# Thirty-two bytes less behind the vector table: where the tiles of a four-sublayer trunk begin in SBUF

## The chip, the cores and the metric

The kernel runs on one core of a Trainium2 chip. What counts is the device time of one execution in microseconds. Below, PE is TensorE's matmul row, PEld its weight-load row, DVE is VectorE, ACT is ScalarE, POOL is GpSimd and SP is the engine that issues most DMAs. SBUF has 128 partitions, and an address in this text is a byte offset within one partition.

## The reference

Two residual layers over a sequence of 1024 tokens with 1024 channels, each with a token mixer and then an MLP of hidden width 4096:

```python
for i in range(DEPTH):                      # DEPTH = 2
    hn = rmsnorm(x, mix_pre_g[i])
    if i % 2 == 0:
        y = pool_mixer(hn, pool_w[j], pool_b[j], pool_scale[j])
    else:
        y = mlstm_mixer(hn, ...)            # 8 heads of 128, chunkwise
    x = x + rmsnorm(y, mix_post_g[i])
    hn = rmsnorm(x, ffn_pre_g[i])
    a = relu(hn @ mlp_w1[i])                # 1024 -> 4096
    y = (a * a) @ mlp_w2[i]                 # 4096 -> 1024
    x = x + rmsnorm(y, ffn_post_g[i])
```

All arrays are float32. Nearly all arithmetic lies in the two MLPs and in the input and output projections of the mLSTM mixer.

## The kernel before, in words

Channels lie on partitions and tokens along the free dimension, in two halves of T = 512 tokens. A product of a 128x128 weight tile with a 128x512 activation tile is made in three **rounded** matmuls. Both operands are split into a high part, rounded to the type float32r, and a low part, the rest, of the same type; the products high·high, weight high with activation low, and weight low with activation high are added in one PSUM bank:

```python
c = row + cols_of(k)
a, b = w_hi[:, c:c + P], w_lo[:, c:c + P]
nc.tensor.matmul(o, a, hi(t), start=(k == 0), stop=False)
nc.tensor.matmul(o, a, lo(t), start=False, stop=False)
last = nc.tensor.matmul(o, b, hi(t), start=False, stop=(k == n - 1))
```

The first operand behind the output is the stationary one (the weights, loaded by a weight load of its own before every matmul), the second is the moving one: 512 columns of 4 bytes, 2048 bytes of each partition in one unbroken run. The same three-matmul pattern stands in `three_passes` (lines 803 to 805, most projections of the mLSTM and the pooling map), `plain_first` (903 to 905), `plain_second` (926 to 928), `pairs_first` (970 to 972, the first MLP matrix as a Strassen-like product of seven), `second` (1020 to 1022, the second MLP matrix likewise), and in the output projection (867 to 869 and 1040 to 1042).

ACT makes the high parts by casts, DVE the low parts by a subtraction, each one step ahead of PE; semaphores keep the order. A ring of four 512-column rows in `w_hi` and `w_lo` holds the weights. SP loads weights into `raw`, `raw_odd` and the `w2` tiles. PE's program order is written out by hand.

A smaller number of matmuls are **plain** float32 ones: the windows of the pooling mixer (line 837), sums of squares with a matrix of ones (785, 792, 814, 1188), transposes (1076, 1090, 1093, 1132), the attention-like products of the mLSTM (1096, 1107, 1118, 1122), and additions through the identity at the end (1196, 1199). A plain float32 matmul leaves two records on PE in the profile, a rounded one leaves one.

**Where the tiles lie.** Tiles are placed in SBUF one behind the other in the order in which they are made, and each takes its size rounded up to a multiple of 32 bytes. The first ones are, in order:

```python
y = [sb(f"y{h}", [P, KT, T]) for h in range(HALVES)]
raw = sb("raw", [P, RAW * BLK])
w_hi = sb("w_hi", [P, ROWS * T], F32R)
w_lo = sb("w_lo", [P, ROWS * T], F32R)
vecs = sb("vecs", [P, VECS])
consts = sb("consts", [P, CONSTS])
...
eps = sb("eps", [P, 1])
```

`y0`, `y1`, `raw`, `w_hi` and `w_lo` begin at 8320, 24704, 41088, 49280 and 57472, all multiples of 64 (of 128, too). `vecs` (169 columns, 676 bytes, in a place of 704) begins at 65664, and `consts` at 66368, also multiples of 64. `eps`, one column of 4 bytes in a place of 32, begins at 68928, and so everything behind it begins at 32 more than a multiple of 64, from `early_h` and `h_plain` (68960) over `x11_hi` (90080), `x11_lo` (98272) and the other activation tiles `x.._hi` and `x.._lo` to `hid_hi` and `hp_hi` (155616), `h_hi` (196576) and `h_lo` (202720). The exceptions stand behind smaller odd-sized tiles: `ssq`, `rs`, `prob` (210176), `hnorm`, `state`, `rows`, `cols` and `small` begin at multiples of 64. All moving operands of all rounded matmuls are slices of 2048 bytes in tiles that begin at 32 more than a multiple of 64. All their stationary operands, in `w_hi` and `w_lo`, begin at multiples of 64.

Of the plain matmuls, the moving operand is `consts` in the transposes and `y` in line 1199 (multiples of 64), and `x_last`, `qT`, `relu_sq`, `win`, `inter_b` and `sq` (32 more) in lines 1196, 1096, 785 and 837. A name in the profile stands as output<-moving,stationary; `state` in line 837 begins at a multiple of 64 as well.

Of the kernel before, what the change touches and what calls it, by code (L numbers as in the profile page):

```python
# [13 lines left out]
P = 128  # L14
# [71 lines left out]
VECS = 169  # L86
# [157 lines left out]
def build(nc, x_in, x_tokens, weights, w_first, w_second, vecs_in, consts_in, bands_in, out):  # L244
# [9 lines left out]
    with ExitStack() as ctx:  # L254
        def sb(name, shape, dt=F32):
            return ctx.enter_context(nc.sbuf_tensor(name, shape, dt))
# [9 lines left out]
        raw = sb("raw", [P, RAW * BLK])  # L266
        w_hi = sb("w_hi", [P, ROWS * T], F32R)
        w_lo = sb("w_lo", [P, ROWS * T], F32R)
        vecs = sb("vecs", [P, VECS])
        consts = sb("consts", [P, CONSTS])  # L270
        ident = consts[:, C_IDENT:C_IDENT + P]
        mask = consts[:, C_MASK:C_MASK + T]
        eps = sb("eps", [P, 1])

        with ExitStack() as shared:
            h_plain = shared.enter_context(nc.sbuf_tensor("h_plain", [P, 2, T], F32))
# [2261 lines left out]
```

## Time and profile before

| | |
|---|---|
| median of 2 runs | 1941.2 us (1939.57 to 1942.83) |
| span of the profiled execution, first to last instruction | 1938.4 us |
| median less that span | 2.8 us |
| granted TensorE clock | 1.000 of full |
| PE, PEld, DVE, ACT busy | 99%, 79%, 69%, 55% of the span |
| chain that ended last | PE 90%, DVE 6%, issue 2%, ACT 2% |

The profile does not give a time of the profiled execution beside its span; the runs' times are taken from outside the program, so the 2.8 us hold what lies around the span and the difference of one execution from another. A sum made against the span is carried over to the median by adding them. Matmuls are pipelined, and their ends in the profile are modelled: the time that one takes from the others is the distance from its start to the next start, not its duration.

### The profile page before, as it was taken

The page shows a single profiled execution, that of the slowest core. Times are in us where ns is not written, and L with a number is a line of the kernel's source. Part 1 is how long each engine was busy: PE and PEld are TensorE (multiplying, and loading weights), DVE is VectorE, ACT ScalarE, POOL GpSimd, SP SyncE. Part 2 cuts the span into 40 slices and gives each one's busy share as a digit, 9 for nine tenths or more (in the row PEclk, how much of TensorE's full clock was granted, in tenths as well). Part 3 has the DMA queues.
Part 4 walks back from the last instruction along what each step waited for, and adds up shares of the span by engine and source line. Part 5 has one row for each costly group of instructions (what it writes and reads, how often), then busy time and mean ns, then how long its engine had stood idle before and what let it go on. Part 6 is the DMA issues. An engine that isn't in the chain of part 4 may idle for free.

```text
span 1938.4 us, 24458 instructions
## 1 busy us (share of the span) xinstructions
PE 1914.3 (99%) x8526; PEld 1534.2 (79%) x8526; DVE 1344.2 (69%) x2120; ACT 1068.5 (55%) x1825; POOL 89.8 (5%) x121
## 2 busy tenths in 40 slices
PE   9999999999999999999999999999999999999999
PEld 6678888888788788888878878777888888878876
DVE  5877565655678987786866868777665656577875
ACT  7655545454445537766766757655555555444533
POOL 0110000000000200010000100020000000000010
PEclk9999999999999999999999999999999999999999
DMA  5344343448633533352323442245243436753353
GB/s 211 122 152 161 120 166 134 159 172 320 218 93 95 181 123 103 109 169 93 99 86 98 133 150 88 77 157 190 77 179 120 179 120 250 281 179 94 108 190 125
DMA packets 79706, 285.00 MB, mean 147 GB/s; under 512 B 9408, under 2 KB 9536, under 8 KB 71136
## 3 DMA queue, kind: packets, MB, share of 16 engines
q1 hardware_dynamic: 64288, 239.96, 35.2%
q0 software_dynamic: 8320, 27.27, 4.3%
q10 hardware_dynamic: 6976, 16.21, 2.7%
q8 instruction: 69, 1.13, 0.3%
q14 instruction: 53, 0.43, 0.1%
HBM read 211.51 MB, written 71.89 MB: 146 GB/s over the span
## 4 chain that ended last, share of the span: by engine, by line
PE 90%; DVE 6%; issue 2%; ACT 2%; DMA 0%; SPq 0%; DVEq 0%; ACTq 0%
PE bank L803 7%; PE bank L805 6%; PE bank L804 6%; PE core L1020 5%; PE core L1021 5%; PE core L1022 5%; PE core L972 5%; PE core L971 5%; PE core L970 5%; PE bank L1020 4%; PE bank L1022 4%; PE bank L1021 4%; PE bank L972 4%; PE bank L971 4%; PE bank L970 4%; PE bank L903 2%
## 5 line engine op out<-in xcount | busy, mean ns | idle before, releaser
L1467 ACT CAST h_hi<-h_raw 128x512 fp32r<-128x512 f32 x188 | 116.5, 620 | 246.7 <-PE core L1022 149.1
L1831 DVE TENSOR_TENSOR w_lo<-raw,w_hi 128x1024 fp32r<-128x1024 f32 x132 | 161.3, 1223 | 125.5 <-ACT w_hi L1281 123.4
L803 PE MATMUL bank<-x_hi,w_hi 128*128 128x512 f32 x560 | 227.3, 406 | 2.9 <-issue 2.5
L1281 ACT CAST w_hi<-raw 128x1024 fp32r<-128x1024 f32 x132 | 137.9, 1045 | 156.9 <-PE bank L805 48.5
L805 PE MATMUL bank<-x_hi,w_lo 128*128 128x512 f32 x560 | 221.8, 396 | 0.0
L804 PE MATMUL bank<-x_lo,w_hi 128*128 128x512 f32 x560 | 220.6, 394 | 0.0
L2088 DVE TENSOR_TENSOR h_lo<-h_raw,h_hi 128x512 fp32r<-128x512 f32 x188 | 129.7, 690 | 120.8 <-ACT h_hi L1467 120.5
L1020 PE MATMUL core<-h_hi,w_hi 128*128 128x512 f32 x464 | 183.8, 396 | 0.6 <-DVE y L2154 0.6
L1021 PE MATMUL core<-h_lo,w_hi 128*128 128x512 f32 x464 | 183.4, 395 | 0.0
L1022 PE MATMUL core<-h_hi,w_lo 128*128 128x512 f32 x464 | 183.0, 394 | 0.0
L1982 DVE TENSOR_TENSOR w_lo<-sums,w_hi 128x512 fp32r<-128x512 f32 x104 | 71.8, 690 | 100.4 <-ACT w_hi L1309 97.5
L1020 PE MATMUL bank<-h_hi,w_hi 128*128 128x512 f32 x336 | 132.9, 395 | 0.0
L1021 PE MATMUL bank<-h_lo,w_hi 128*128 128x512 f32 x336 | 132.8, 395 | 0.0
L1022 PE MATMUL bank<-h_hi,w_lo 128*128 128x512 f32 x336 | 132.5, 394 | 0.0
L2126 DVE TENSOR_TENSOR w_lo<-w,w_hi 128x512 fp32r<-128x512 f32 x174 | 123.6, 711 | 11.1 <-ACT w_hi L1483 6.7
L803 PEld LDWEIGHTS bank<-x_hi,w_hi 128*128 128x128 f32 x560 | 105.3, 188 | 27.5 <-issue 5.2
L805 PEld LDWEIGHTS bank<-x_hi,w_lo 128*128 128x128 f32 x560 | 105.1, 188 | 25.5
L804 PEld LDWEIGHTS bank<-x_lo,w_hi 128*128 128x128 f32 x560 | 105.3, 188 | 23.9 <-issue 0.7
L1483 ACT CAST w_hi<-w 128x512 fp32r<-128x512 f32 x174 | 107.1, 615 | 12.3 <-DVE w L2106 4.6
L1309 ACT CAST w_hi<-sums 128x512 fp32r<-128x512 f32 x104 | 64.7, 622 | 82.1 <-PE core L972 37.9
L1020 PEld LDWEIGHTS core<-h_hi,w_hi 128*128 128x128 f32 x464 | 87.1, 188 | 23.2 <-issue 2.2
L1022 PEld LDWEIGHTS core<-h_hi,w_lo 128*128 128x128 f32 x464 | 87.1, 188 | 21.4
(334 smaller groups left out, 4397.5 us busy)
## 6 DMA issues: line engine op xcount, KB each, us to landing
raw<-weights SPq DMA_DIRECT2D x132, 512.0 KB, 3.3
h_pair_dram<-y SPq DMA_DIRECT2D x26, 1792.0 KB, 6.6
h_raw<-h_pair_dram SPq DMA_DIRECT2D x182, 256.0 KB, 2.8
w<-second_pairs SPq DMA_DIRECT2D x24, 768.0 KB, 4.5
raw_odd<-first_pairs SPq DMA_DIRECT2D x14, 1024.0 KB, 7.2
x_scratch<-y POOLq DMA_DIRECT2D x48, 256.0 KB, 2.4
raw<-first_pairs SPq DMA_DIRECT2D x12, 1024.0 KB, 7.1
xold<-x_scratch POOLq DMA_DIRECT2D x40, 256.0 KB, 3.4
```

What stands on the lines that cost most here:

```text
L803: nc.tensor.matmul(o, a, hi(t), start=(k == 0), stop=False)
L804: nc.tensor.matmul(o, a, lo(t), start=False, stop=False)
L805: last = nc.tensor.matmul(o, b, hi(t), start=False, stop=(k == n - 1))
L970: nc.tensor.matmul(o, a, xh[:, k, :], start=(fresh and k == 0), stop=False, skip_group_check=True)
L971: nc.tensor.matmul(o, a, xl[:, k, :], start=False, stop=False, skip_group_check=True)
L972: last = nc.tensor.matmul(o, b, xh[:, k, :], start=False, stop=(final and k == 3), skip_group_check=True)
L1020: nc.tensor.matmul(o[:, :], a, hh, start=(fresh and first), stop=False, skip_group_check=True)
L1021: nc.tensor.matmul(o[:, :], a, hl, start=False, stop=False, skip_group_check=True)
L1022: ins = nc.tensor.matmul(o[:, :], b, hh, start=False, stop=(final and last), skip_group_check=True)
L1281: nc.scalar.copy(w_hi[:, ROW[u] * T:(ROW[u] + 2) * T], raw[:, (n % RAW) * BLK:(n % RAW + 1) * BLK]).then_inc(hi_ready, 1)
L1831: dve.tensor_tensor(w_lo[:, s], raw[:, (n % RAW) * BLK:(n % RAW + 1) * BLK], w_hi[:, s].bitcast(F32), ALU.subtract).then_inc(lo_ready, 1)
L2088: dve.tensor_tensor(lo, h_raw[:, at % H_RAW, :], hi.bitcast(F32), ALU.subtract).then_inc(h_lo_ready, 1)
```

## The change

`eps` loses its tile and becomes the 170th column of the vector table. 170 columns are 680 bytes, which still take a place of 704, so `consts` stays where it is, and every tile behind the place of `eps` begins 32 bytes lower.

```diff
         w_lo = sb("w_lo", [P, ROWS * T], F32R)
-        vecs = sb("vecs", [P, VECS])
+        vecs_eps = sb("vecs", [P, VECS + 1])
+        vecs, eps = vecs_eps[:, 0:VECS], vecs_eps[:, VECS:VECS + 1]
         consts = sb("consts", [P, CONSTS])
         ident = consts[:, C_IDENT:C_IDENT + P]
         mask = consts[:, C_MASK:C_MASK + T]
-        eps = sb("eps", [P, 1])
```

After it `early_h` begins at 68928, `x11_hi` at 90048, `hid_hi` at 155584, `h_hi` at 196544 and `h_lo` at 202688: all multiples of 64. `y`, `raw`, `w_hi`, `w_lo`, `vecs` and `consts` stay. `ssq`, `rs`, `prob`, `hnorm`, `state`, `rows`, `cols` and `small`, which began at multiples of 64, begin at 32 more. On PE, DVE, ACT, POOL and SP the same instructions stand in the same order with the same waits; only the address of what they read and write differs, and what read `eps` (the biases of the square roots, and the memset at line 1259) now names `vecs`.

## Rows read from the trace of the kernel before

**Rows 1.** The page: busy time and share of each engine; the chain that ended last.
```profile
PE 1914.3 (99%) x8526; PEld 1534.2 (79%) x8526; DVE 1344.2 (69%) x2120; ACT 1068.5 (55%) x1825; POOL 89.8 (5%) x121
...
PE 90%; DVE 6%; issue 2%; ACT 2%; DMA 0%; SPq 0%; DVEq 0%; ACTq 0%
```

**Rows 2.** The longest wait of PE by releaser: us, times, longest.
```profile
PE bank L803 <- issue: 3.5, 4, 1.5
```

**Rows 3.** PE's instructions with w_lo, whole span: us, busy (count), clock, DMA share, GB/s.
```profile
0.00:1938.50 1938.50, 1001.95 (x2528) 1.00 0.43 147
```

**Rows 4.** The same of PE's instructions with w_hi.
```profile
0.00:1938.50 1938.50, 1596.14 (x5056) 1.00 0.43 147
```

**Rows 5.** Timeline of PE from 600.76: start us, us, engine line op tiles.
```profile
600.76 0.39 PE L1020 MATMUL bank<-h_hi,w_hi 128*128 128x512 f32 x1
...
604.96 0.39 PE L1020 MATMUL bank<-h_hi,w_hi 128*128 128x512 f32 x1
```

**Rows 6.** PE in two long stretches, columns as in group 3.
```profile
150.00:600.00 450.00, 450.00 (x1929) 1.00 0.46 166
1350.00:1700.00 350.00, 350.00 (x1501) 1.00 0.47 175
```

**Rows 7.** Timeline of PE at the program's end, plain float32, 512 columns.
```profile
1925.43 0.59 PE L1196 MATMUL bank<-x_last,consts 128*128 128x512 f32 x1
1925.86 2.74 PE L1196 MATMUL core<-x_last,consts 128*128 128x512 f32 x6
1928.43 2.81 PE L1199 MATMUL bank<-y,consts 128*128 128x512 f32 x6
...
1930.22 1.02 PE L1199 MATMUL bank<-y,consts 128*128 128x512 f32 x2
```

**Rows 8.** Timeline of PE, plain float32, 128 columns.
```profile
809.41 0.60 PE L1090 MATMUL core<-consts,kT 128*128 128x128 f32 x4
809.85 0.60 PE L1093 MATMUL core<-consts,vT 128*128 128x128 f32 x4
810.28 1.06 PE L1096 MATMUL core<-qT,kT 128*128 128x128 f32 x8
```

**Rows 9.** Timeline of PE in the pooling windows.
```profile
18.23 0.38 PE L837 MATMUL core<-sq,y 128*128 128x128 f32 x2
```

**Rows 10.** Groups by form: line, tiles, count | busy us, mean ns of one | idle before.
```profile
L1096 PE MATMUL core<-qT,kT 128*128 128x128 f32 x128 | 16.9, 275 | 0.0
...
L1090 PE MATMUL core<-consts,kT 128*128 128x128 f32 x64 | 9.6, 273 | 0.1
```

**Rows 11.** Timeline of PE from 700.01.
```profile
700.01 0.40 PE L1020 MATMUL core<-h_hi,w_hi 128*128 128x512 f32 x1
700.25 0.39 PE L1021 MATMUL core<-h_lo,w_hi 128*128 128x512 f32 x1
700.48 0.39 PE L1022 MATMUL core<-h_hi,w_lo 128*128 128x512 f32 x1
700.71 0.40 PE L1020 MATMUL core<-h_hi,w_hi 128*128 128x512 f32 x1
```

**Rows 12.** Groups by form of the first MLP matrix, columns as in group 10.
```profile
L972 PE MATMUL core<-x_hi,w_lo 128*128 128x512 f32 x224 | 89.4, 399 | 0.0
L971 PE MATMUL core<-x_lo,w_hi 128*128 128x512 f32 x224 | 88.2, 394 | 0.0
L970 PE MATMUL core<-x_hi,w_hi 128*128 128x512 f32 x224 | 87.8, 392 | 0.0
```

**Rows 13.** PE's instructions with w_lo where PE has gaps, columns as in group 3.
```profile
0.00:112.00 112.00, 34.91 (x88) 1.00 0.49 173
1250.00:1315.00 65.00, 31.93 (x81) 1.00 0.42 140
```

**Rows 14.** Busy PE, PEld, DVE, ACT and POOL (count of each), clock, DMA share, GB/s.
```profile
629.70:648.80 19.10, 19.10 (x83) 15.39 (x82) 18.30 (x23) 9.13 (x16) 5.29 (x5) 1.00 0.45 135
...
600.00:700.00 100.00, 99.69 (x427) 79.91 (x427) 87.37 (x124) 49.85 (x86) 14.97 (x18) 1.00 0.48 150
```

## The prediction, made before the changed kernel ran

> **What bounds the kernel now.** I began with the engines' busy times and the chain of waits [rows 1]: PE is busy for 99% of the span and the chain that ended last runs through PE for 90% of it, with 6% on DVE and 2% on ACT. The waits of PE by their releaser [rows 2] are short, 3.5 us for the longest group. So a change that makes a matmul shorter is paid out nearly in full, and one that touches another engine's work hardly at all.
>
> Next I counted. Every rounded matmul reads either `w_lo` or `w_hi`: 2528 [rows 3] and 5056 [rows 4] records, 7584 in all, of 8526 on PE. All have 512 columns, and all have a moving operand whose place the change moves from 32 beyond a multiple of 64 bytes to a multiple of 64.
>
> Then the time that one takes, from start to start. From 600.76 to 604.96 us there are 18 steps between starts [rows 5]: 4.20 us / 18 = **233.3 ns**. The long stretches agree: 450 us hold 1929 and 350 us hold 1501 rounded matmuls [rows 6], 233.3 and 233.2 ns, at a granted clock of 1.00, which is the 2.4 GHz level. 7584 x 233.3 ns = 1769 us of the 1938.4 us span. This is the figure that the change can move, and it does not depend on what ACT, DVE or the DMAs do beside it, since it holds over stretches with very different neighbours.
>
> What should it be? The plain float32 records give a measure. With 512 columns they follow each other at 2.57 us / 6 = 429 ns [rows 7] (1925.86 to 1928.43), with 128 columns at 0.44 us / 4 = 109 ns [rows 8]. The difference, 320 ns for 384 columns, is 0.833 ns a column, two cycles of 2.4 GHz, and some 2.4 ns remain for each record whatever its length. A rounded matmul that takes one cycle a column would need 512 x 0.4167 + 2.4 = **215.7 ns**. It takes 233.3 ns, **17.6 ns** more. The plain ones, which load weights for every record as well, show no such surplus. The question of this case is how much of those 17.6 ns comes from where the moving operand begins.
>
> The page "TensorE: Matmul & The Clock Gate" of the Trainium skill (Part 2 and Back-to-back issue gap) gives the gap at full clock as columns / 2.4 plus 2.5 ns, about 216 ns here, with the weights read through a port of their own. The trace agrees for the plain records (two cycles a column in place of one) and does not for the rounded ones, at 233.3 ns; the page names no cause for such a surplus.
>
> **The change, part by part.**
>
> *The moving operands of 7584 rounded matmuls go from 32 to 0 modulo 64.* No row shows a rounded matmul with a moving operand at a multiple of 64, so the cost is bounded from both sides. The bound of most gain is the whole surplus, 17.6 ns each: 7584 x 17.6 = 133.5 us. The bound of no gain comes from the plain records: `x_last` (32 modulo 64) and `y` (0 modulo 64) as moving operands, both against `consts`: 429 ns, and 1.02 us for two records less the 0.59 us that the last one lasts, 430 ns [rows 7]. With 128 columns, `sq` (32 modulo 64) takes 0.38 less 0.27, some 110 ns, beside 109 for `consts` (0 modulo 64) [rows 8 to 10]. The place makes no difference there. But plain records take a column in two cycles, and so ask for their 2048 bytes at half the rate: a lost read could hide in them and not in a rounded matmul.
>
> Between these ends one value has a mechanism that the rows suggest. The starts in a trio of rounded matmuls are not even: 0.24, 0.23, 0.23 us from 700.01 to 700.71 [rows 11], and in the first MLP matrix one of the three is always longer, 399 ns beside 392 and 394 [rows 12]. The slip is 5 to 7 ns, and 16 columns x 0.4167 = 6.67 ns: 16 columns of 4 bytes are 64 bytes. 233.3 ns is 560 cycles, 35 times 16. So I read the stream as coming in blocks of 64 bytes, at one block for 16 cycles. A run of 2048 bytes that begins on a block touches 32 of them, and one that begins in the middle of a block touches 33. The change would then take one block of 35 from each rounded matmul, **6.67 ns**, leaving 226.7 ns. This is an estimate; the two blocks that stay (switching weights, or what else) have nothing to do with the place. 7584 x 6.67 = **50.6 us**.
>
> I take this value, though the nearest row by kind is the plain one with no difference, because the plain ones run at half the rate, and the excess of the rounded ones appears exactly where the read rate is doubled.
>
> *What is not paid out.* Up to 112 us, and from 1250 to 1315 us, PE has gaps and ends on ACT's and DVE's steps; there stand 3 x (88 + 81) = 507 rounded matmuls [rows 13], whose gain I count as lost: 507 x 6.67 = 3.4 us. From 629.7 to 648.8 us DVE is busy for 18.30 of 19.10 us [rows 14], and the same stretch comes back in the second MLP. PE could be 2.9% faster there, 0.55 us, twice 0.55 is 1.1 us; DVE leaves 0.8 us of room, so it would be just enough, but waits between engines stand in the way, and I count it as lost. In the wider stretch, 600 to 700, DVE has 87.37 us in 100 [rows 14], enough room. Elsewhere DVE and ACT work at 69% and 55% of the span, and a PE that is 2.9% faster brings them to 71% and 57%.
>
> *The tiles that go from 0 to 32 modulo 64* (`prob`, `hnorm`, `state`, `rows`, `cols`, `small`): moving or stationary operands of plain matmuls, and operands of DVE and ACT. By the plain rows above, nothing; `qT` against `kT`, both at 32, shows the largest difference of any plain pair: (1.06 - 0.275) / 7 = 112 ns against 109 [rows 8, 10]. If all 942 other records became 3 ns longer it would be 2.8 us; `state` and `prob` stand in a quarter of them, so at most 0.7 us. I take 0, and keep that in the range.
>
> *`eps` inside `vecs`*: the same instructions with the same waits; its memset and the load of the other 169 columns touch different bytes. Nothing.
>
> **The sum**, against the profiled execution: 1938.4 - 50.6 + 3.4 + 1.1 = 1892.3 us of span, and with the 2.8 us between span and median 1895.1. **1895 us**, 2.4% less.
>
> **The rivals.**
>
> *A, no difference.* The surplus of 17.6 ns belongs to the rounded format or to the switch of weights, and the place of the moving operand is as indifferent as in the plain records [rows 7]. The time would be 1941 us. For it speaks that every pair of plain records that differs in the place alone takes the same time, and that the rounded matmuls switch weights at every step. Against it: the plain ones switch weights as often, even at 109 ns [rows 8], without a surplus. The page "SBUF — State Buffer" of the Trainium skill (Specifications) gives lines of 16 bytes; with lines of 16, or of 32, both places begin on a line, and the change would do nothing, which is this rival's 1941 us. No run shown here tells a line's length.
>
> *B, the whole surplus goes.* Each block of 64 bytes that is cut in two costs something, not only the one at the end, and a run on the blocks streams at one column a cycle. 7584 x 17.6 = 133.5 us, less 507 x 17.6 = 8.9 us where PE waits, and less what DVE then holds back: in each of the two dense stretches of 19.1 us PE would want 1.4 us and DVE leaves 0.8 [rows 14], and waits of PE for DVE that are hidden today come out at stage ends, some 3 us in all by the size of those in [rows 2]. 1941.2 - 133.5 + 8.9 + 3 = 1819.6, **1820 us**. For it: 215.7 ns is what the plain records lead to. Against it: nothing explains 42 cycles by one misplaced start, and the slip that the trace shows is some 16 cycles.
>
> *C, slower.* The stationary operands `w_hi` and `w_lo` begin at multiples of 64, and now the moving ones do too. If the weight load for the next matmul and the moving stream meet in the same half of the same block at the same time, each matmul loses a block: 7584 x 6.67 = +50.6 us, **1992 us**. It decides from 5.1 ns a matmul on (2% of 1941 over 7584). Against it stand `y` against `consts`, both at multiples of 64, with 430 ns [rows 7], no more than `x_last`, and `consts` with 109 ns [rows 8]; for it, that `qT` and `kT`, which share their place modulo 64, are the only pair at 112.
>
> **How the numbers follow.** The block estimate 0.36, A 0.33, B 0.24, C 0.07. The likeliest gives 1895 us. A measurement of this kernel can tell about 2% from no change, so the limits are 1902 and 1980 us. The block estimate and B are faster; I leave 0.02 of the first for the case that more is held back than 4.5 us: faster 0.58, within 2% 0.35, slower 0.07. The range reaches from B with some 5 us less held back, 1815 us, to A with the 0.7 us of the moved small tiles and the spread of the runs, 1946 us; it leaves out C and a little of B. The likeliest case alone has 1885 to 1902 us. It is wide because the price of one nanosecond a matmul is 7.6 us, and no row of this trace shows a rounded matmul at the other place.
>
> **What would show each step right or wrong.** In the changed kernel's timeline the distance between starts of rounded matmuls in long stretches answers everything: 226.7 ns (450 us would hold 1985) for the block estimate, 233.3 (1929) for A, 215.7 (2086) for B, 240 (1875) for C. If the trio's uneven steps are gone, the reading by blocks is supported. The plain records should stay at 429 and 109 ns; if `x_last` gets shorter, the plain ones depend on the place too. PE's waits should grow only before 112 us, around 630 to 650 and around 1250 to 1315 us, and by less than 5 us. I would be wrong as a whole if the distance fell and the time did not: then DVE or ACT would be the bound in more places than [rows 14] shows.

## The result, and the profile after

| | before | changed |
|---|---|---|
| median of 2 runs | 1941.2 us (1939.57 to 1942.83) | 1916.7 us (1916.18 to 1917.21) |
| span of the profiled execution | 1938.4 us | 1914.4 us |
| ratio of the times | | 0.9877, 95% interval 0.986 to 0.9894 |

The changed kernel is 1.2% faster, 24.5 us. The forecast was 1895 us with a range of 1815 to 1946. The direction was right; about half of the gain came.

The page of the changed kernel, busy times and chain, beside [rows 1]:

```profile
PE 1883.8 (98%) x8526; PEld 1535.6 (80%) x8526; DVE 1343.7 (70%) x2120; ACT 1067.9 (56%) x1825; POOL 89.8 (5%) x121
...
PE 87%; DVE 8%; issue 2%; ACT 2%; DMA 0%; SPq 0%; DVEq 0%; ACTq 0%
```

DVE's and ACT's busy times are the same to 0.6 us. All of the change is on PE. Its long stretches, beside [rows 6] (us, busy and count, clock, DMA share, GB/s):

```profile
150.00:590.00 440.00, 439.96 (x1922) 1.00 0.47 170
1340.00:1660.00 320.00, 320.00 (x1399) 1.00 0.45 170
```

440 us / 1922 is 228.9 ns and 320 / 1399 is 228.7 ns (the counts take in a matmul or two at the edges). From the starts themselves a rounded matmul now takes 229.0 ns, where it took 233.3: **4.3 ns less**, not 6.67. The timeline of the changed kernel shows it too, beside [rows 5]:

```profile
592.38 0.39 PE L1020 MATMUL bank<-h_hi,w_hi 128*128 128x512 f32 x1
...
595.81 0.39 PE L1020 MATMUL bank<-h_hi,w_hi 128*128 128x512 f32 x1
```

Fifteen steps, 3.43 us, 228.7 ns each. The uneven steps within a trio, which were to go if the reading by blocks was right, are still there: 226, 229 and 232 ns in turn, where before they were 231, 232 and 237. The plain records stay as they were: `x_last` from 1901.83 to 1904.41 us has six in 2.58 us, 430 ns each, and the transposes of line 1090 take 0.44 us for four. But one kind of rounded matmul did not gain, and that is the line of this trace to stop at. `early_h` too begins at a multiple of 64 now:

```profile
430.66 0.39 PE L1020 MATMUL bank<-early_h,w_hi 128*128 128x512 f32 x1
...
432.75 0.40 PE L1020 MATMUL bank<-early_h,w_hi 128*128 128x512 f32 x1
```

Nine steps of PE in 2.09 us are 232 ns; the trios of such matmuls lasted 699 to 701 ns before and last 697 to 703 now, while those with any other tile went from 700 to 687. Seventy-two matmuls are worth nothing in the time, but they say that a start at a multiple of 64 is not enough.

### The profile page after: what moved, and what is told of

The parts are those of the page before. It is cut to its first block, busy times and chain, and to the rows that moved or that the text cites. A ratio compares the mean times of both kernels' runs of the same rounds, so it can differ in the third digit from the quotient of the medians.

```text
span 1914.4 us, 24458 instructions
## 1 busy us (share of the span) xinstructions
PE 1883.8 (98%) x8526; PEld 1535.6 (80%) x8526; DVE 1343.7 (70%) x2120; ACT 1067.9 (56%) x1825; POOL 89.8 (5%) x121
## 3 DMA queue, kind: packets, MB, share of 16 engines
q8 instruction: 69, 1.13, 0.3%
## 4 chain that ended last, share of the span: by engine, by line
PE 87%; DVE 8%; issue 2%; ACT 2%; DMA 0%; SPq 0%; DVEq 0%; ACTq 0%
PE bank L803 6%; PE bank L805 5%; PE bank L804 5%; PE core L1020 5%; PE core L1022 5%; PE core L1021 5%; PE core L971 5%; PE core L970 5%; PE core L972 5%; PE bank L1020 4%; PE bank L1022 4%; PE bank L1021 4%; PE bank L971 4%; PE bank L970 4%; PE bank L972 4%; PE bank L903 2%
## 5 line engine op out<-in xcount | busy, mean ns | idle before, releaser
L1021 PEld LDWEIGHTS core<-h_lo,w_hi 128*128 128x128 f32 x464 | 87.1, 188 | 19.2
```

What stands on the lines that cost most here:

```text
L1021: nc.tensor.matmul(o[:, :], a, hl, start=False, stop=False, skip_group_check=True)
```

## The experiments

**1. Where must a moving operand begin?** The trunk is left out of this kernel; each case has a line of its own, for instance

```diff
+ [mm(bank[0][:, 0:512], W(128 + (z == 2) * 8192, 128 * (j % 4)), M(64 + (z == 1) * 8192, 512),
+     start=(j == 0 and z == 0), stop=(j == 15 and z == 2)) for j in range(16) for z in range(3)]
```

where `W` and `M` slice the weights and the moving operand at a byte offset, both counted from a multiple of 2048.

> This kernel leaves the whole trunk out (it copies its input to its output) and only times matmuls, each case in its own line: trios of rounded 128x512 matmuls as in the kernel (weights high with moving high, weights high with moving low, weights low with moving high, the low parts 8192 bytes behind the high ones, weights stepping by 512 bytes from 128 beyond a multiple of 2048), with the moving operand beginning 0, 32, 64 to 2016 bytes beyond a multiple of 2048; then the stationary operand moved, fewer columns, starts off multiples of 32, one operand pair repeated, plain float32 and bfloat16. Theory 1 (multiples of 64 decide): 229 ns a matmul at every even multiple of 32, 233.3 at every odd one, whatever the place in 2048. Theory 2 (where the 2048-byte run crosses a boundary of 2048 decides, since the tiles that gained begin 64 bytes before one and early_h, which begins 1344 beyond one, did not gain): 233 to 234 ns over most of the 64 places, 229 only near 1984, and something else again at 0, where nothing is crossed. Theory 3 (a clash of the moving stream with the weight load): the time changes when only the stationary operand is moved. Per-column or per-matmul: with 128, 256 and 384 columns the surplus over columns x 0.4167 ns stays at 15 to 18 ns if it is a price of the matmul, and shrinks in proportion if it is one of the columns. Plain float32 429 ns at each place.

The timeline of that kernel (start us, us, line, tiles, count). Lines 53 to 61 have the moving operand at 0, 32, 64 to 256, with the weights at 128; the distance between two starts over 48 is the time of one matmul:

```profile
38.17 11.32 PE L53 MATMUL bank<-mov,wts 128*128 128x512 f32 x48
49.33 11.40 PE L54 MATMUL bank<-mov,wts 128*128 128x512 f32 x48
60.57 11.37 PE L55 MATMUL bank<-mov,wts 128*128 128x512 f32 x48
71.77 11.36 PE L56 MATMUL bank<-mov,wts 128*128 128x512 f32 x48
82.97 11.07 PE L57 MATMUL bank<-mov,wts 128*128 128x512 f32 x48
93.87 11.37 PE L58 MATMUL bank<-mov,wts 128*128 128x512 f32 x48
105.08 11.16 PE L59 MATMUL bank<-mov,wts 128*128 128x512 f32 x48
116.07 11.37 PE L60 MATMUL bank<-mov,wts 128*128 128x512 f32 x48
127.28 11.36 PE L61 MATMUL bank<-mov,wts 128*128 128x512 f32 x48
```

At 0 and 64, both multiples of 64, a matmul takes 11.16 / 48 = 232.5 and 11.20 / 48 = 233.3 ns; at 128 it takes 10.90 / 48 = 227 ns; at 192, where the changed kernel's tiles lie if whole multiples of 256 are left out, 10.99 / 48 = 229 ns. The pattern comes back every 256 bytes up to 2016, within about 1 ns (the start at 256 has 233.5 where that at 0 has 232.5). So theories 1 and 2 fall: what counts is neither a multiple of 64 nor the boundary of 2048. In the second part only the weights are moved, under a moving operand that stays:

```profile
751.12 11.06 PE L117 MATMUL bank<-mov,wts 128*128 128x512 f32 x48
762.02 11.35 PE L118 MATMUL bank<-mov,wts 128*128 128x512 f32 x48
773.21 11.36 PE L119 MATMUL bank<-mov,wts 128*128 128x512 f32 x48
784.41 11.40 PE L120 MATMUL bank<-mov,wts 128*128 128x512 f32 x48
...
883.75 11.08 PE L129 MATMUL bank<-mov,wts 128*128 128x512 f32 x48
894.67 11.35 PE L130 MATMUL bank<-mov,wts 128*128 128x512 f32 x48
```

Lines 117 to 120 have the moving operand at 0 and the weights at 0, 32, 64 and 96: 227, 233, 233, then 234 ns. Line 129 has both at 32, at no multiple of 64, and takes 10.92 / 48 = 227 ns. Theory 3 is left, that the two operands' places act together. For starts at multiples of 32 what counts is the **distance, start of the moving operand less start of the weights, modulo 256**. By it all of the kernel's rows fall into place: 96 before (233.4 ns), 64 after (228.8 here, 229.0 in the whole kernel), and for `early_h` 224 before and 192 after (233.3 both). Means of the middle spacings of each case, from the starts of both this kernel and the one of experiment 3:

```
distance modulo 256   0      32     64     96     128           160    192    224
ns a matmul           226.7  233.3  228.8  233.4  232.4, 233.5  234.3  233.3  233.3
```

At distance 128 the two values come from different starts in the first kernel; the start at 256 gave 233.5 there and 232.4 in the other, so 1 ns can hang on what ran before.

Two kinds showed no dependence at the places tried. Plain float32 at 0, 32 and 1984 (distances 128, 160 and 64), lines 191 to 193, and bfloat16, line 195:

```profile
1506.31 20.76 PE L191 MATMUL bank<-mov,wts 128*128 128x512 f32 x48
1526.91 20.76 PE L192 MATMUL bank<-mov,wts 128*128 128x512 f32 x48
1547.51 20.76 PE L193 MATMUL bank<-mov,wts 128*128 128x512 f32 x48
...
1588.93 10.31 PE L195 MATMUL bank<-mb,wb 128*128 128x512 bf16 x47
```

20.60 / 48 = 429.2 ns at each, and 215.8 ns for bfloat16. Plain float32 was not tried at distance 0.

The question per column or per matmul got neither of its two answers: the surplus over columns x 0.4167 ns was 58 ns with 128 columns (111.7 ns at every place tried), 7 to 13 with 256 and 13 to 17 with 384. With 256 columns the good distance is another one. Line 170 has distance 192:

```profile
1290.63 5.61 PE L170 MATMUL bank<-mov,wts 128*128 128x256 f32 x48
1296.08 8.61 PE L171 MATMUL bank<-mov,wts 128*128 128x384 f32 x48
```

That is 5.45 / 48 = 113.5 ns, where distance 0 takes 120.0 (experiment 3).

**2. The same in the whole kernel.** Three placements, each with all of the trunk and nothing else changed. In the first, on the kernel before, `eps` goes ahead of `w_hi`, so that the weights move and no moving tile does:

```diff
+        eps = sb("eps", [P, 1])
         w_hi = sb("w_hi", [P, ROWS * T], F32R)
...
         consts = sb("consts", [P, CONSTS])
...
-        eps = sb("eps", [P, 1])
```

> The kernel before with eps ahead of w_hi in place of behind consts: the weights begin 32 bytes higher and every moving tile stays where it was, 32 beyond a multiple of 64. Theory 'multiples of 64': nothing is gained, 233.3 ns a rounded matmul, 1941 us. Theory 'distance' (what counts is the start of the moving operand less the start of the stationary one, modulo 256: 96 before, 64 in the changed kernel): the distance is now 64, so 229 ns and 1917 us, as the changed kernel.

In the second, on the changed kernel, the tiles stay at multiples of 64 and the distance is made a bad one:

```diff
+        pool_bs = sb("pool_bs", [P, KT])
+        ssq = sb("ssq", [P, 2, HALVES * CPH])
+        rs = sb("rs", [P, HALVES * CPH])
         w_hi = sb("w_hi", [P, ROWS * T], F32R)
...
         ones = sb("ones", [P, P])
-        pool_bs = sb("pool_bs", [P, KT])
-        ssq = sb("ssq", [P, 2, HALVES * CPH])
-        rs = sb("rs", [P, HALVES * CPH])
```

> The changed kernel with pool_bs, ssq and rs (128 bytes) ahead of w_hi: the moving tiles of the arena stay where the change put them, at multiples of 64, and the weights too are at multiples of 64, 128 bytes higher. Theory 'multiples of 64': 229 ns, 1917 us as the changed kernel. Theory 'distance': it is 192 modulo 256, at which the scan had 233.3 ns, so 1941 us as before.

In the third, also on the changed kernel, it is made 0 for all, `early_h` included: `ssq` alone ahead of `w_hi`, `pool_bs` and `rs` ahead of `early_h`.

> The changed kernel with ssq (64 bytes) ahead of w_hi and pool_bs and rs (64 bytes) ahead of early_h: all moving tiles of rounded matmuls, early_h too, have the distance 0 modulo 256 to the weights. Theory 'distance': 226.7 ns a rounded matmul, 2.3 ns less than the changed kernel, 7584 x 2.3 = 17 us, less what PE's waits take back: 1900 us. Theory 'multiples of 64': 1917 us.

And in a fourth, run later, 0 for all with no operand at a multiple of 64: `eps` and `ssq` ahead of `w_hi`, on the kernel before, and `pool_bs` and `rs` ahead of `early_h`.

> The kernel before with eps and ssq (96 bytes) ahead of w_hi, and pool_bs and rs (64) ahead of early_h: the distance of every moving tile of a rounded matmul to the weights is 0 modulo 256, as in e_same256, but weights and moving tiles all begin 32 beyond a multiple of 64. If the distance alone counts: 226.7 ns and 1901 us, as e_same256. If starts at multiples of 64 give anything beside it: more than that, up to 1941 us.

| kernel | starts modulo 64: weights, moving | distance | us | ratio to before, 95% interval |
|---|---|---|---|---|
| before | 0, 32 | 96 | 1940.0 (with the first three), 1939.8 (with the fourth) | |
| changed | 0, 0 | 64 | 1916.7 | 0.9877 (0.986 to 0.9894) |
| eps ahead | 32, 32 | 64 | 1914.5 | 0.9866 (0.985 to 0.9883) |
| 128 bytes ahead | 0, 0 | 192 | 1939.9 | 1.0005 (0.9996 to 1.0015) |
| all at 0 | 0, 0 | 0 | 1901.4 | 0.9804 (0.9789 to 0.9818) |
| all at 0, odd | 32, 32 | 0 | 1902.7 | 0.9808 (0.9791 to 0.9824) |

The changed kernel's row is that of the first section, beside a before of 1941.2 us.

Each of the four came out within 3 us of what the distance gave and against what multiples of 64 gave. The windows say the same in counts. With 128 bytes ahead:

```profile
150.00:600.00 450.00, 450.00 (x1929) 1.00 0.45 165
```

which is the very count of [rows 6], and with all at distance 0:

```profile
150.00:590.00 440.00, 439.93 (x1941) 1.00 0.47 168
```

440 / 1941 = 226.7 ns. `early_h` gains there as well (the second line below is the first matmul of another tile, and five steps lie between the two, 1.13 us, 226 ns each):

```profile
426.65 0.39 PE L1021 MATMUL bank<-early_h,w_hi 128*128 128x512 f32 x1
...
427.78 0.39 PE L1020 MATMUL bank<-h_hi,w_hi 128*128 128x512 f32 x1
```

The kernel with all at 0 is 2.0% faster than before. It is the version to keep: 1901.4 us stand against the changed kernel's 1916.7, though the two were not timed side by side; the intervals of their ratios to before do not touch.

**3. What is it that meets?** A second kernel of matmuls alone:

> Only matmuls, as in the first scan; the trunk is left out. (a) The distance from stationary to moving start in steps of 8 bytes from 0 to 248: 226.7 ns at 0, 229 at 64 and 233 to 234 at most others, if the scan's values hold. (b) Two weights in turn, with distance 0 to the moving operand of their own matmul and 32 or 224 to that of the matmul before, during which they are loaded, and the reverse: if the load of the next weights clashes with the running stream, the pair with distance 0 to the next weights takes 226.7 and the other 233; if a matmul's own weights count, the reverse. (c) 96, 64 and 32 weight columns: if the surplus comes from the weight load beside the stream, it shrinks with the columns loaded, towards 215.8 ns, and so does its dependence on the distance; if it is a price of the rounded format or of switching weights, it stays. (d) Weights 2048, 4096 and 6144 bytes further: no change. (e) 256 to 448 columns: the dependence on distance is the same number of ns at each.

(a) held in the main: 226.7 ns at 0, 228.8 at 64 and 233 to 234 at most others. Finer distances gave values between and beyond: 230.0 ns at 56, 104 and 248, 240.0 at 120 and 236.7 at 240. The 240 of the timeline, line 68, beside its neighbours at 112 and 128:

```profile
206.08 11.25 PE L67 MATMUL bank<-mov,wts 128*128 128x512 f32 x48
217.17 11.68 PE L68 MATMUL bank<-mov,wts 128*128 128x512 f32 x48
228.68 11.31 PE L69 MATMUL bank<-mov,wts 128*128 128x512 f32 x48
```

(11.51 / 48 = 239.8 ns.) Nothing was faster than distance 0. Off the multiples of 32 the period of 256 is not clean: at distance 112 this kernel has 231.1 ns, with the moving operand 240 beyond a multiple of 2048, and the first one 226.7, with it at 2032; at 120 they have 240.0 and 234.3. Tiles begin at multiples of 32, so the trunk does not meet these. (d) held: weights 2048, 4096 and 6144 bytes further take 226.7 ns each. (c) fell in its first part. With fewer weight columns the surplus did not shrink towards 215.8 ns:

```profile
463.26 11.20 PE L90 MATMUL bank<-mov,wts 128*96 128x512 f32 x48
474.30 11.04 PE L91 MATMUL bank<-mov,wts 128*96 128x512 f32 x48
...
573.85 11.28 PE L100 MATMUL bank<-mov,wts 128*32 128x512 f32 x48
584.97 11.34 PE L101 MATMUL bank<-mov,wts 128*32 128x512 f32 x48
```

With 96 columns it is distance 0 that takes 230.0 ns (line 90, 11.04 / 48) and distance 32 that takes 226.7 (line 91); with 32 columns 231.7 and 233.3. What did shrink is the dependence on the distance. Over the same five distances (0, 32, 64, 96 and 160) the values run from 226.7 to 234.3 ns with 128 weight columns, from 226.7 to 233.3 with 96, from 228.4 to 231.4 with 64 and from 230.5 to 233.3 with 32. So the surplus does not come down with the weights loaded, but how many are loaded changes how much the distance matters and which distance is the good one. (e), the same number of ns at each length, fell. In ns, at distances 0, 64 and 96:

```
columns    256     320     384     448     512
at 0       120.0   146.7   173.3   202.6   226.7
at 64      117.8   146.7   173.3   200.0   228.8
at 96      119.9   146.7   176.7   205.3   233.4
columns x 0.4167
           106.7   133.3   160.0   186.7   213.3
```

At 320, 384, 448 and 512 columns the lowest is columns x 0.4167 + 13.3 ns, 32 cycles of 2.4 GHz for each rounded matmul. It is no floor for every length: 256 columns go down to 113.3 ns (mean of line 170's middle spacings), 6.7 above 106.7. What comes on top of the 13.3 ns in this table is 0 to 7 ns, and hangs on the distance at 384, 448 and 512 columns and not at 320. At 448 columns distance 64 is better than 0. (b), whether a matmul's own or the next weights belong to its distance, was not decided: 231.7 ns for one order and 230.0 for the other. A third kernel asked again:

> Only matmuls, the trunk is left out. Weights and moving operand change in turn, 128 bytes beyond a multiple of 256 or x more, to see which two starts belong together. If a matmul's time hangs on its moving operand and its own weights: the cases with own distance 0 give 226.7 for each x. If on the moving operand and the next weights: those with next distance 0 do. If on both, or on the moving operand after: neither does, as in the two cases of the scan before (231.7 and 230.0). The moving operand alternating over the same weights, and the weights over one moving operand, should then lie between the values at the two distances. bfloat16 over eight distances: 215.8 at each, if the clash needs 4-byte operands at full rate. 352, 416 and 480 columns: columns x 0.4167 + 13.3 ns at distance 0, if 32 cycles are paid once a matmul.

"Neither" it was. With own distance 0 and the pair moved by 32, 64, 96, 128, 160, 192 and 224 bytes in turn a matmul takes 231.7, 231.9, 234.0, 228.3, 234.1, 231.8 and 233.4 ns; with next distance 0 230.0, 231.5, 230.0, 230.0, 230.0, 231.6 and 230.0. Nor do the one-sided cases lie between their two ends: with the weights at rest and the moving operand in turn at distances 0 and 192 the mean is 226.7 ns, where a steady 192 costs 233.3. The spacings are patterns of four, 228, 225, 229, 225 there. With the moving operand at rest and the weights in turn at distances 0 and 224 the mean is 234.9, above both ends. A matmul's time thus hangs on a history of starts, not on one pair. bfloat16 takes 215.8 ns at each of the eight distances tried (the trace lacks single records in some of them), and 352, 416 and 480 columns took 161.2, 188.3 and 216.7 ns at distance 0, which is 1.2, 1.6 and 3.4 above the rule of 13.3 ns, and 162.2, 193.3 and 220.0 at 96. The rule that I expected there was met at none of the three.

## Why the prediction was right, and where it failed

*The number.* The sum gave 1892.3 us of span and 1914.4 was measured, 22.1 more: 7584 x (6.67 - 4.3) = 18.0 us because a matmul gained less, and 8.6 - 4.5 = 4.1 us because more was held back. The range reached from 1815 to 1946 us and so took in no change at all; that the time lies in it says little. The band of the likeliest case alone, 1885 to 1902 us, was missed.

*What bounds the kernel* held. PE's matmuls set the time, 7584 of them count, and a change in their spacing is paid out for three quarters.

*The surplus of 17.6 ns* over a cycle a column was read rightly off the plain records, and it is real: bfloat16 shows the 215.8 ns in the same kernel. It has two parts. 11 ns of it stay at every placement tried: 32 cycles above the columns where bfloat16 has 6. The rest depends on placement: 6.7 ns in the kernel before, and at most 7.6 (234.3 at distance 160) at the distances that tiles at multiples of 32 can have.

**The step that failed** is the one on the block: "a run of 2048 bytes that begins on a block touches 32 of them, and one that begins in the middle of a block touches 33". Three runs go against it: with the moving operand still at 32 modulo 64 as much was gained when the weights moved instead, at multiples of 64 it gained nothing with the distance 192, and `early_h` gained nothing in the changed kernel. Its term was 6.67 ns and measured 4.3, and the agreement in sign is luck: a shift by 32 bytes took the distance from 96 to 64, one of the two good values of eight. The same shift from 0 would have cost 6.6 ns. The 6.67 ns are, as it happens, the whole step from 233.3 to 226.7 at distance 0, but a grain of 16 cycles is not shown: 228.8 ns are 549 cycles and 230.0 are 552, neither a multiple of 16.

*The bound of no gain from the plain records* misled in the other way. `x_last` and `y` do take the same 429 ns, and so do plain matmuls at the four distances tried (64, 96, 128 and 160); the reservation, that they ask for their bytes at half the rate, was the part worth keeping. That the rate is the reason is not shown: what is shown is that at the distances tried only float32r, of three formats, is sensitive.

*Rival C*, a meeting of weights and moving stream, named the right pair of operands with the wrong sign: it had equal places as the bad case, and they are the best one. The argument against it in the text used plain records, which are not sensitive. *Rival A* was wrong, though the kernel with 128 bytes ahead shows a case in which it would have been right to about a microsecond. *Rival B* fell: no placement comes near 215.7 ns.

*What is not paid out* was put at 4.5 us for a gain of 6.67 ns, and was 8.6 us for one of 4.3: 7584 x 4.3 = 32.6 us, and the span fell by 24.0. Matching each matmul's start in the two traces, 3.3 us are lost between 740 and 1235 us, in the heads, where I had counted nothing; 1.9 between 1280 and 1313; 2.4 up to 170; 0.6 in the two dense stretches of DVE, near the 1.1 that I had. The waits of the changed kernel, beside [rows 2]:

```profile
PE core L926 <- issue: 5.2, 3, 2.2
PE core L1132 <- DVE hnorm L2290: 3.9, 5, 1.7
PE bank L803 <- issue: 3.9, 4, 1.8
```

Before, the first two were 3.0 and 2.4 us. The step that was short is "Elsewhere DVE and ACT work at 69% and 55%": the share of busy time said that there is room. But the transpose of line 1132 waits at the end of a chain of small DVE and ACT steps that does not get shorter: from the start of line 2262 on DVE to the end of line 2290 it is 4.97 us in both kernels (797.53 to 802.50 before, 787.12 to 792.09 after). Four times in the heads PE now comes 0.2 to 0.5 us sooner to it, 1.5 us in all, and another 1.0 us lies in front of line 803. The room on an engine is not room in a chain.

*The tiles that went from 0 to 32 modulo 64* were put at nothing, and that held: 648 spacings between plain matmuls in the heads add up to 72.22 us before and 72.28 after.

*The other waits.* Of the 1.9 us between 1280 and 1313, 1.4, and of the 2.4 up to 170, 1.9, have another source, which "issue" hides. This is the longest wait of line 926 in the changed kernel, with DVE beside it:

```profile
111.43 0.69 DVE L1910 TENSOR_TENSOR y<-xold,step_t 128x512 f32<-128x512 f32 x1 [2.21 <-DMA xold<-x_tiles]
112.27 1.23 DVE L1831 TENSOR_TENSOR w_lo<-raw,w_hi 128x1024 fp32r<-128x1024 f32 x1
...
113.59 0.47 PE L926 MATMUL core<-hp_hi,w_hi 128*128 128x512 f32 x1 [2.24 <-issue]
```

DVE waits 2.2 us for the DMA that brings `xold`, and only behind that makes the low weights that PE needs; PE starts 0.09 us behind their end. How long DVE waits there is not set by the matmuls: near 110 us it was 2.47 us before and 0.96 in the kernel with 128 bytes ahead, whose matmuls have the same spacing, and in the one with `eps` ahead, with the spacing of the changed one, DVE did not wait there but 2.33 us at 1295. In the changed kernel it waits 1.40 us at 1298, where the kernel before has no such wait at the same step. So these pauses are a matter of when that DMA lands, and the sum had no term for it. Behind the one at 111 us stands a stretch of half clock, told below.

## What to carry to other kernels

Where PE is the bound and streams rounded float32, measure the spacing of starts in one long stretch and, at 512 columns, compare it with columns x 0.4167 + 13.3 ns; if it is above, shift the weights against the moving tiles by multiples of 32 bytes and look again. In this kernel's pattern (128 weight columns, 512 moving) equal starts modulo 256 were best, and placing a few small tiles elsewhere was enough. With other widths another distance can be best: 192 for 256 moving columns, 64 for 448, 32 for 96 weight columns. These are the best of the few tried, so the offsets are to be measured for the pattern at hand. And when a shift helps, look for a tile that was shifted and did not gain: it tells which rule is at work.

## What was unexpected in the hardware

The dependence on distance itself, 226.7 to 240.0 ns for the same matmul, in float32r alone of the three formats tried, with a period of 256 bytes where the starts are multiples of 32.

The clock, too. In the changed kernel PE stood still a little longer in front of the first `plain_second` matmul of another bank, from the one that began at 110.95 us to the next at 113.59, where before it was 111.56 to 113.94. Its granted clock in the microseconds behind it:

```profile
110.00:114.00 4.00, 1.76 (x8) 1.00 0.25 95
114.00:115.00 1.00, 1.00 (x5) 0.70 0.44 139
115.00:116.00 1.00, 1.00 (x3) 0.50 0.81 295
116.00:117.00 1.00, 1.00 (x4) 0.50 0.41 164
117.00:118.00 1.00, 1.00 (x4) 0.60 0.00 0
```

Half is the 1.2 GHz level, for 3.4 us, and matmuls follow each other there at 427 ns:

```profile
115.19 0.63 PE L928 MATMUL core<-hp_hi,w_lo 128*128 128x512 f32 x1
115.61 0.63 PE L926 MATMUL core<-hp_hi,w_hi 128*128 128x512 f32 x1
```

The kernel before had no such stretch before its end. The pause, 0.3 us longer, and this stretch, some 1.6 us, make up 1.9 of the 2.4 us lost up to 170 us. The other traces bear on whether the longer pause brought it. In the six whole kernels three pauses between two starts of PE are longer than 2.4 us: this one of 2.64, one of 2.84 in the kernel with all at 0, and one of 3.07 in the one with `eps` ahead:

```profile
1294.37 0.40 PE L928 MATMUL bank<-hp_hi,w_lo 128*128 128x512 f32 x1
1297.44 0.57 PE L926 MATMUL core<-hp_hi,w_hi 128*128 128x512 f32 x1 [2.67 <-issue]
...
1298.00:1299.00 1.00, 1.00 (x4) 0.50 0.53 127
```

Behind each of the three, and nowhere else before the program's end, the clock stood at half for 3.4 us. Behind the shorter pauses, up to the 2.37 us of the kernel before, it did not fall. That is three cases of three; no run lengthens the pause alone.

**Open.** Why distance matters: no run separates a shared read path from any other meeting of the two streams, and which of the neighbouring starts count is not settled. That the 13.3 ns belong to the float32r format and not to loading 4-byte weights is not settled either; fewer weight columns did not lower them. All of the spacings come from one traced execution of each kernel.
